# Long convolution of a mixer block by odd frequencies, with time split by four

## The chip, the core and the metric

The kernel runs on one core of one Trainium2 chip. The metric is the device time of one execution in microseconds; the median of three runs before the change is 1589.33 us (1589.04 to 1589.37). Engines: TensorE (PE: matmul; PEld: its weight loads), VectorE (DVE), ScalarE (ACT), GpSimd (POOL) and SyncE (SP, which issues nearly all DMAs). They run side by side and order themselves by semaphores.

## The reference

Two blocks in a row on 512 tokens of width 1024, all in float32. The first has two layers (gated attention, then retention, each with a memory cross-attention). The second mixes the tokens by a gated long convolution (half of its width) and by gated linear attention (the other half), and then runs an MLP. What the change touches is the long convolution, its filter spectrum, and the two norms in a row between the blocks:

```python
def _long_conv(u, spec, bias):
    length = u.shape[1]                      # 512
    uf = u.astype(jnp.float32)
    y = jnp.fft.irfft(jnp.fft.rfft(uf, n=2 * length, axis=1) * spec, n=2 * length, axis=1)[:, :length]
    return (y + uf * bias.astype(jnp.float32)).astype(u.dtype)

def _hyena_gate_conv(u, spec, bias):
    x0, x1, v = jnp.split(u, 3, axis=-1)
    return x0 * _long_conv(x1 * v, spec, bias)

# in _hyena_spectrum: h is the learned filter, 512 taps forward (h[:, 0]) and 512 backward (h[:, 1])
    kern = jnp.concatenate([h[:, 0], jnp.zeros((1, D_HYENA), f32), h[:0:-1, 1]], axis=0)
    kern = kern * lax.rsqrt(jnp.sum(kern * kern, axis=0, keepdims=True) + EPS)
    return jnp.fft.rfft(kern, axis=0)

# first_block ends with rmsnorm(x, final_norm_g); second_block begins with _rms_norm of that
```

## The kernel before, in words

Activations lie transposed: features on the 128 partitions, 512 tokens along the free axis. Every projection walks through the weight matrices in tiles of 128 x 1024 that SP loads into `raw`, three tiles deep behind the split. A float32 product is made of three fp32r products: ACT rounds a weight tile to its high half `wh`, and POOL (or, for the tiles listed in `DVE_LOW`, DVE) makes the low half `wl = raw - wh`; activations are split in the same way (`HH`, `HL`). `features` (L492) then runs per 128 output columns eight matmuls with `wh`, waits for `wl` ("low"), and runs four with it. `unit_f` is two such tiles, 48 matmuls of 512 columns. `feed.take()` and `feed.split_next()` fix, on every engine alike, at which place in its own instruction stream a tile is split: the order on each engine is written out by hand, and each engine works strictly in that order.

Around the change the order on PE is: the last projection of the first block; the transform of the filter (`phases("filter", ...)`, L902 to L919) with the two sums of squares for the norms between them; the units `hx1 0`, `hv 0`, `hx1 1`, `hv 1`, `hx0 0` (projections of the convolution's three inputs, with the turning of u = x1 * v in between); the transform of u for frequencies 0 to 127 (`phases("u", ..., 0, ...)`); the context's sum of squares; unit `hx0 1`; the transform of u for frequencies 128 to 255; the units `og 0` and `gq 0`; the inverse transform (L956 to L966); the gate columns (`slot_gates`, L969, which write banks 4 and 5); and `both_k`, which runs 24 matmuls on the latent tokens and then 24 on the context into bank 4. The latter wait until ACT has copied the gate columns out of bank 4 (`GR`, L2665).

The transform treats even and odd tokens apart (two phases, cosine and sine each), so the filter's and u's transforms are 48 matmuls each, plus four one-row matmuls for the highest frequency. ACT and DVE copy the filter's spectrum to `KS`. DVE then multiplies u's spectrum, which it reads straight from PSUM (`banks`), with `KS` (L1874), adds parts, and POOL adds the rest (L2986, L2988) into `Y`, from which PE takes the inverse: 32 plain float32 matmuls of 256 columns, which the trace shows as 64 records. Behind the products DVE's stream goes on with the context's second norm (`normed("ctx", ...)`: `T<-CX,gxc,R`, then `CL`), ACT's with its high half `CH`, then the splits of the next weight tiles, then `hyena_out(0..3)` (which frees the banks 4 to 7 of the inverse), then `GR`.

The norm between the blocks: ACT makes 1/sqrt of the first sum (`R`), DVE squares it and multiplies the second sum, ACT takes the second 1/sqrt, DVE multiplies the two to `R2`.

Of the kernel before, what the change touches and what calls it, by code (L numbers as in the profile page):

```python
# [8 lines left out]
ALU = mybir.AluOpType  # L9
# [15 lines left out]
QSCALE = 1.0 / math.sqrt(128.0)  # L25
LOGS, TANHS = "natural_log_exp_and_others", "exp_and_others"
# [238 lines left out]
def build(nc, a, out, stack):  # L265
# [49 lines left out]
    one = eps[:, 1:2]  # L315
# [52 lines left out]
    FTH, FTL = at("FTH", [128, 4, 2, 256], 124, F32R), at("FTL", [128, 4, 2, 256], 132, F32R)  # L368
    FTR, IT = at("FTR", [128, 4, 2, 256], 60), at("IT", [128, 2, 2, T], 132)
# [3 lines left out]
    KS = at("KS", [128, 8, T], 140)  # L373
# [7 lines left out]
    TM = [at("TM%d" % n, [128, T], 116 + 2 * n) for n in range(4)]  # L381
# [86 lines left out]
    def tensor(pe):  # L468
# [418 lines left out]
        def phases(tag, x_cos, x_sin, ft, banks, which=range(4)):  # L887

            for n in which:
                (xh, xl), cs, k0 = ((x_cos, 0, 0), (x_cos, 0, 2), (x_sin, 1, 0), (x_sin, 1, 2))[n]  # L890
                b, c = banks[n], slice(128 * ft, 128 * ft + 128)
                pe.wait_ge(done("dft high", 1), *free[b])
                for k in (k0, k0 + 1):
                    mm(bank[b], FTH[:, k, cs, c], xh[:, k, :], k == k0, False)
                    mm(bank[b], FTH[:, k, cs, c], xl[:, k, :], False, False)
                pe.wait_ge(done("dft low"))
                for k in (k0, k0 + 1):
                    i = mm(bank[b], FTL[:, k, cs, c], xh[:, k, :], False, k == k0 + 1)
                i.then_inc(*by_pe("spectrum", tag, ft, n))

        pe.wait_ge(done("energy", 3), done("taps low", 3))
        phases("filter", (URH, URL), (USH, USL), 0, SP_BANKS[0], (0, 1))  # L902
        feed.split_next()
        pe.wait_ge(done("squared", "x2"), *free[6])
        mm(bank[6], ones[:, :], ACC[:, :], True, True).then_inc(*by_pe("sum", "x2"))
        free[6] = (done("sum kept", "x2"),)
        pe.wait_ge(done("squared", "x2 gf"), *free[7])
        mm(bank[7], ones[:, :], ACC2[:, :], True, True).then_inc(*by_pe("sum", "x2 gf"))
        free[7] = (done("sum kept", "x2 gf"),)
        phases("filter", (URH, URL), (USH, USL), 0, SP_BANKS[0], (2, 3))  # L910
        phases("filter", (URH, URL), (USH, USL), 1, SP_BANKS[1])
        for ft in range(2):
            for n in range(4):
                free[SP_BANKS[ft][n]] = (done("spectrum kept", ft, n),)
        pe.wait_ge(*free[4])
        for k in range(2):
            mm(bank[4][0:1, :], FTH[:, k, 1, 0:1], URH[:, k, :], k == 0, False)
            i = mm(bank[4][0:1, :], FTH[:, k, 1, 0:1], URL[:, k, :], False, k == 1)
        i.then_inc(*by_pe("even sum"))  # L919
        free[4] = (done("even sum kept"),)  # L920

        def turn_u(c):
            b = 2 + c
            pe.wait_ge(done("u", c), *free[b])
            for k in range(4):
                ut = UT[:, c, :].rearrange("p (n two) -> p two n", two=2)[:, k // 2, 128 * (k % 2):128 * (k % 2) + 128]
                i = turn(bank[b][:, 128 * k:128 * k + 128], ut)
            i.then_inc(*by_pe("u turned", c))
            free[b] = (done("uk", c),)
# [13 lines left out]
        phases("u", (UKH, UKL), (UKH, UKL), 0, HY_BANKS[0])  # L943
        pe.wait_ge(done("squared", "ctx"), *free[4])
        mm(bank[4][:, 0:256], ones[:, :], ACC[:, 0:256], True, True).then_inc(*by_pe("sum", "ctx"))
        free[4] = (done("sum kept", "ctx"),)
        for b in HY_BANKS[0]:
            free[b] = (done("product", 0),)
        unit_f(("hx0", 1))
        phases("u", (UKH, UKL), (UKH, UKL), 1, HY_BANKS[1])  # L950
        for b in HY_BANKS[1]:
            free[b] = (done("product", 1),)
        feed.split_next()
        unit_f(("og", 0), (2, 3))
# [280 lines left out]
    def vector(dve):  # L1235
# [152 lines left out]
        eng.memset(eps[:, 0:1], 1e-6).then_inc(*by_dve())  # L1388
# [341 lines left out]
        def dft_low():  # L1730
            dve.wait_ge(done("dft"), done("half", ("out", 1, 3), 1, 1))
            for i in range(2):
                dve.wait_ge(done("dft high", i))
                tt(FTL[:, 2 * i:2 * i + 2, :, :], FTR[:, 2 * i:2 * i + 2, :, :], FTH[:, 2 * i:2 * i + 2, :, :].bitcast(F32),
                   ALU.subtract).then_inc(*by_dve("dft low"))

        def filter_norm():
            dve.wait_ge(done("energy scale"))
            ts(chs, chs, 4.0 / 1024.0, None, ALU.mult).then_inc(*by_dve("filter scale"))
# [11 lines left out]
        project_out(1, steps)  # L1751
        x2_done = by_dve.last()
# [9 lines left out]
        def keep_spectrum(ft):  # L1762
            for n in (1, 3):
                dve.wait_ge(done("spectrum", "filter", ft, n))
                eng.tensor_copy(KS[:, 4 * ft + n, :], bank[SP_BANKS[ft][n]]).then_inc(*by_dve("spectrum kept", ft, n))

        def normed(tag, src, gain, scale, n, bias, xh, xl):


            def low(k):  # L1770
                t = temp("normed", tag, k)
                dve.wait_ge(done("h", tag, k), done("even sum") if tag == "x2" and k > 3 else None)
# [14 lines left out]
        t = turn("second scale")  # L1787
        dve.wait_ge(done("scale", "x2"), temp_free("second scale"))
        tt(t[:, :], R[:, :], R[:, :], ALU.mult).then_inc(*by_dve())
        dve.wait_ge(by_dve.last(), done("sum", "x2 gf"))  # L1790
        tt(t[:, :], bank[7], t[:, :], ALU.mult).then_inc(*by_dve("sum kept", "x2 gf"))
        keep_spectrum(0)
        dve.wait_ge(done("second scale"))
        tt(R2[:, :], R2[:, :], R[:, :], ALU.mult).then_inc(*by_dve())
        dve.wait_ge(by_dve.last(), x2_done)
        normed("x2", X, gfx, R2, T, mod, HH, HL)
        keep_spectrum(1)
        dve.wait_ge(done("even sum"), done("spectrum kept", 0, 2))
        eng.tensor_copy(KS[0:1, 2, :], bank[4][0:1, :]).then_inc(*by_dve("even sum kept"))
        def scale_x(ks):  # L1800
            for k in ks:
                stt(X[:, k, :], X[:, k, :], P("gf", k), R[:, :], ALU.mult, ALU.mult).then_inc(*by_dve())
# [45 lines left out]
        tm = [0]  # L1848

        def product(ft, banks):  # L1850

            even_c, odd_c, even_s, odd_s = (bank[b] for b in banks)
            kec, koc, kes, kos = (KS[:, 4 * ft + n, :] for n in range(4))
            dve.wait_ge(*(done("spectrum kept", ft, n) for n in range(4)), done("even sum kept"), done("even sum"))
            for n, parts in ((2, ((even_c, kes, 0), (even_s, kec, 2), (odd_c, kos, 1), (odd_s, koc, 3))),
                             (3, ((even_c, kos, 0), (even_s, koc, 2), (odd_c, kes, 1), (odd_s, kec, 3))),
                             (0, ((even_c, kec, 0), (odd_c, koc, 1), (even_s, kes, 2), (odd_s, kos, 3))),
                             (1, ((even_c, koc, 0), (odd_c, kec, 1), (even_s, kos, 2), (odd_s, kes, 3)))):
                y, made, t = Y[:, 4 * ft + n, :], [], []
                for i, (b, k, from_phase) in enumerate(parts):  # L1860
                    if i == 2 and n % 2 == 0:
                        dve.wait_ge(*made)
                        tt(y, y, t[0], ALU.add).then_inc(*by_dve("y half", ft, n))
                    dve.wait_ge(done("spectrum", "u", ft, from_phase))
                    if i == 0:
                        x = y
                    else:
# [1473 lines left out]
```

## Time and profile before

| | us |
|---|---|
| median of the runs (3) | 1589.33 |
| the profiled execution, own time | 1589.16 |
| its span (first to last instruction) | 1587.4 |
| PE busy | 1578.8 (99%) |
| DVE busy | 995.3 (63%) |
| ACT busy | 725.2 (46%) |
| POOL busy | 602.6 (38%) |

Busy times are sums over the instructions of one engine, with overlaps taken once. Matmuls are pipelined: a record of 0.39 us starts 0.23 us after the one before it, so PE's pace is read from the starts. The result of a matmul reaches the other engines at the end of its record.

### The profile page before, as it was taken

How to read it: one execution, taken by the hardware profiler on the slowest of the kernel's cores; microseconds unless marked ns; L12 is line 12 of the kernel's file. 1: busy time of each engine (PE TensorE's matmuls, PEld its weight loads, DVE VectorE, ACT ScalarE, POOL GpSimd, SP SyncE). 2: the span in 40 equal slices, each digit the busy share in tenths (PEclk: the TensorE clock that was granted, in tenths of full speed). 3: DMA queues.
4: the chain of work that ended last, by engine and by line, in shares of the span. 5: the costliest groups of instructions: out<-in, count | busy, mean ns of one | idle time of the engine just before them, and what ended most of it. 6: DMA issues, size and time to landing. Idle time of an engine off the chain costs nothing.

```text
span 1587.4 us, 21833 instructions
## 1 busy us (share of the span) xinstructions
PE 1578.8 (99%) x8864; PEld 1360.0 (86%) x8864; DVE 995.3 (63%) x1479; ACT 725.2 (46%) x1116; POOL 602.6 (38%) x301
## 2 busy tenths in 40 slices
PE   9999999999999999999999999999999999999998
PEld 7888898889888888888888778889888889999997
DVE  7888867676766365554554676782356885555554
ACT  6533443343433344455555554324434555545454
POOL 1002113221244434455555443353223335555552
PEclk9999999999999999999999999999999999999999
DMA  6554434343466423333333432132111233233321
GB/s 246 171 174 147 141 119 136 117 132 127 121 221 201 164 69 106 102 100 106 107 107 104 148 124 66 54 107 83 41 54 67 80 106 107 94 106 95 105 93 54
DMA packets 54413, 182.69 MB, mean 115 GB/s; under 512 B 6556, under 2 KB 7196, under 8 KB 53928
## 3 DMA queue, kind: packets, MB, share of 16 engines
q1 hardware_dynamic: 54024, 180.76, 34.6%
q8 instruction: 70, 1.15, 0.3%
q10 hardware_dynamic: 288, 0.52, 0.1%
q14 instruction: 31, 0.25, 0.1%
HBM read 174.16 MB, written 3.96 MB: 112 GB/s over the span
## 4 chain that ended last, share of the span: by engine, by line
PE 94%; DVE 4%; DMA 0%; ACT 0%; issue 0%; SPq 0%; POOL 0%; DVEq 0%; ACTq 0%
PE banks L472 92%; PE banks L475 2%; DVE ada L1242 1%; DVE wl L1273 1%; DMA maskf<-cst_dram 0%; DVE WA L1242 0%; DVE TM L1874 0%; ACT Sc L2221 0%; DVE ACC L1309 0%; DVE TM L1884 0%; DVE nmx L1345 0%; POOL wl L2896 0%; DVE Sc L1355 0%; DVE ML L1242 0%; SPq L3072 0%
## 5 line engine op out<-in xcount | busy, mean ns | idle before, releaser
L2896 POOL TENSOR_TENSOR wl<-raw,wh 128x1024 fp32r<-128x1024 f32 x139 | 346.0, 2492 | 383.3 <-ACT wh L2224 383.3
L472 PE MATMUL banks<-HH,wh 128*128 128x512 f32 (+2 forms) x944 | 362.1, 386 | 0.3 <-DVE X L1550 0.3
L472 PE MATMUL banks<-HL,wh 128*128 128x512 f32 (+2 forms) x944 | 352.6, 379 | 0.0
L2224 ACT ACTIVATE wh<-raw 128x1024 fp32r<-128x1024 f32 x246 | 257.2, 1051 | 190.6 <-PE banks L472 182.7
L472 PE MATMUL banks<-HH,wl 128*128 128x512 f32 (+1 forms) x936 | 251.2, 380 | 0.1
L472 PEld LDWEIGHTS banks<-HH,wh 128*128 128x128 f32 (+1 forms) x944 | 177.2, 188 | 37.0 <-issue 2.6
L472 PEld LDWEIGHTS banks<-HL,wh 128*128 128x128 f32 (+1 forms) x944 | 177.0, 188 | 34.5 <-issue 1.2
L472 PEld LDWEIGHTS banks<-HH,wl 128*128 128x128 f32 x936 | 172.1, 188 | 35.0 <-issue 1.5
L472 PE MATMUL banks<-wh,HH 128*128 128x256 f32 x448 | 127.8, 285 | 0.0
L472 PE MATMUL banks<-wl,HH 128*128 128x256 f32 x448 | 126.7, 283 | 0.0
L472 PE MATMUL banks<-wh,HL 128*128 128x256 f32 x448 | 126.7, 283 | 0.0
L1273 DVE TENSOR_TENSOR wl<-raw,wh 128x1024 fp32r<-128x1024 f32 x82 | 100.4, 1237 | 23.5 <-ACT wh L2224 23.5
L472 PE MATMUL banks<-OH,wh 128*128 128x512 f32 x256 | 101.6, 397 | 0.0
L472 PE MATMUL banks<-FLO,wh 128*128 128x512 f32 x256 | 99.8, 390 | 0.0
L472 PE MATMUL banks<-OL,wh 128*128 128x512 f32 x256 | 99.8, 390 | 0.0
L472 PE MATMUL banks<-FHI,wh 128*128 128x512 f32 x256 | 99.7, 390 | 0.0
L2909 POOL TENSOR_TENSOR OL<-T,OH 128x512 fp32r<-128x512 f32 x21 | 28.0, 1335 | 178.4 <-ACT OH L2224 178.4
L472 PEld LDWEIGHTS banks<-wh,HL 128*128 128x128 f32 x448 | 85.7, 191 | 0.5 <-issue 0.2
L472 PEld LDWEIGHTS banks<-wh,HH 128*128 128x128 f32 x448 | 85.7, 191 | 0.5 <-issue 0.2
L472 PEld LDWEIGHTS banks<-wl,HH 128*128 128x128 f32 x448 | 85.7, 191 | 0.0
L2901 POOL TENSOR_TENSOR SL<-WS,SH 128x1024 fp32r<-128x1024 f32 x24 | 57.9, 2412 | 46.1 <-ACT SH L2224 46.1
L2934 POOL TENSOR_TENSOR CM<-CB,mask 128x512 f32<-128x512 f32 x12 | 27.6, 2297 | 124.0 <-DMA CB<-sums_dram 115.8
(441 smaller groups left out, 3262.0 us busy)
## 6 DMA issues: line engine op xcount, KB each, us to landing
raw<-wst_dram SPq DMA_DIRECT2D x294, 512.0 KB, 3.5
X<-xT_dram SPq DMA_DIRECT2D x8, 512.0 KB, 6.0
CB<-sums_dram SPq DMA_DIRECT2D x12, 256.0 KB, 3.1
D<-dec_dram SPq DMA_DIRECT2D x12, 256.0 KB, 2.8
x_dram<-X SPq DMA_DIRECT2D x3, 512.0 KB, 6.7
QS<-QX SPq DMA_DIRECT2D x24, 64.0 KB, 2.8
KSw<-KX SPq DMA_DIRECT2D x24, 64.0 KB, 2.0
X<-x_dram SPq DMA_DIRECT2D x3, 512.0 KB, 4.5
```

The source lines that it names most:

```text
L472: return pe.eng.matmul(dst, w, x, start=start, stop=stop, skip_group_check=True)
L475: return pe.eng.transpose(dst, x, ident[:, :])
L1242: return eng.scalar_tensor_tensor(out=dst, in0=x, scalar=s, in1=y, op0=op0, op1=op1)
L1273: tt(wl[:, q, :], raw[:, i % NRAW, :], wh[:, q, :].bitcast(F32), ALU.subtract).then_inc(*by_dve("low", u))
L2224: return eng.activation(dst, src, ACT.Copy)
L2896: tt(wl[:, q, :], raw[:, i % NRAW, :], wh[:, q, :].bitcast(F32), ALU.subtract).then_inc(*by_pool("low", u))
L2901: tt(SL_[:, v % NS, :], WS[:, v % 2, :], SH_[:, v % NS, :].bitcast(F32), ALU.subtract).then_inc(*by_pool("sums low", u))
L2909: tt(OL[:, tile, :], t[:, :], OH[:, tile, :].bitcast(F32), ALU.subtract).then_inc(*by_pool("l", "o", l, tile))
L2934: tt(CM[:, :].rearrange("p (i m) -> p i m", i=4), CB[:, :].rearrange("p (i m) -> p i m", i=4), mask[:, :].rearrange("p (i m) -> p i m", i= ...
```

## The change

The transform now takes 256 odd frequencies of a length of 2048 half steps, f = 2k + 1, and the tokens in four groups by their number modulo 4. A matmul of one group gives 128 frequencies, and the other 128 follow from sums and differences of the groups. So the filter's transform is 36 matmuls (`spectrum(...)`, one or two groups each) and that of u 24, both before unit `hx0 1`; u's second transform behind `hx0 1` is gone. The inverse is 32 float32 matmuls of 128 columns. In return there are sums and differences ahead of the product and behind it. ACT copies one of two bank pairs to `TM` or `HO`, DVE adds and subtracts (`XP`, `Y`), POOL makes the filter's sums in `KS` (`filter_pair`), the differences `XM` (in `Y`), a part of the last product and the odd parts. The products are made of tiles 1024 long whose two inputs both lie in SBUF (`XP` or `XM`, and `KS`). For the inverse, the groups 0 and 2 of all four channel tiles come first, then 1 and 3.

Unit `hx0 1` writes banks 6 and 7 in place of 0 and 1; the context's sum of squares goes to bank 2, between the halves of `hx0 1`, and is taken out by ACT behind that unit's `conv`. Unit `og 0`, which is next, writes banks 2 and 3.

For the two norms, DVE forms the weighted sum ACC2 + 1e-6 ACC before the sum over partitions, and ACT takes R2 from that one sum (bias 1e-12).

```diff
+        def spectrum(b, *terms):
+            pe.wait_ge(done("dft high"), *free[b])
+            for n, (m, (xh, xl), p) in enumerate(terms):
+                mm(bank[b], FTH[:, m, :], xh[:, p, :], n == 0, False)
+                mm(bank[b], FTH[:, m, :], xl[:, p, :], False, False)
+            pe.wait_ge(done("dft low"))
+            for n, (m, (xh, xl), p) in enumerate(terms):
+                i = mm(bank[b], FTL[:, m, :], xh[:, p, :], False, n == len(terms) - 1)
...
+        pe.wait_ge(done("both squared", "x2"), *free[7])
+        mm(bank[7], ones[:, :], ACC2[:, :], True, True).then_inc(*by_pe("sum", "x2 gf"))
...
+        def context_sum():
+            pe.wait_ge(done("squared", "ctx"), *free[2])
+            mm(bank[2][:, 0:256], ones[:, :], ACC[:, 0:256], True, True).then_inc(*by_pe("sum", "ctx"))
+            free[2] = (done("sum kept", "ctx"),)
+
+        unit_f(("hx0", 1), (6, 7), beside=context_sum)
         feed.split_next()
         unit_f(("og", 0), (2, 3))
         unit_f(("gq", 0))
+        for group in ((0, 2), (1, 3)):
+            for c in range(4):
...
+                for p in group:
+                    pe.wait_ge(done("y", p))
+                    for cs in range(2):
+                        i = mm(bank[b][:, 128 * p:128 * p + 128], Z[p][:, cs, 128 * c:128 * c + 128], IT[:, p, cs, :],
+                               p + cs == 0, p == 3 and cs == 1)
...
+        dve.wait_ge(done("squared", "x2"), done("squared", "x2 gf"))
+        stt(ACC2[:, :], ACC[:, :], EPS, ACC2[:, :], ALU.mult, ALU.add).then_inc(*by_dve("both squared", "x2"))
...
+        def times(sign, b):
+            x, p, q = (XP, XM)[sign], (PP, PM)[sign][:, 2 * b:2 * b + 2, :], TM[:, 2 * b:2 * b + 2, :]
+            h = KS[:, 4 * sign + 2 * b:4 * sign + 2 * b + 2, :]
+            dve.wait_ge(done("h", b), done(("x plus", "x minus")[sign], b))
+            for n, dst in enumerate((p, q)):
                 dve.wait_ge(by_dve.last())
+                tt(dst, x[:, 2 * b + n:2 * b + n + 1, :].to_broadcast([128, 2, T]), h, ALU.mult).then_inc(*by_dve("times", sign, b))
...
         for j in range(2):
-            conv(("hx0", 1), j, j, 2 + j, X0[:, 2 + j, :])
+            conv(("hx0", 1), j, 6 + j, 2 + j, X0[:, 2 + j, :])
+        rstd(done("sum", "ctx"), ("sum kept", "ctx"), ("scale", "ctx"), 2, 256, R[:, 0:256], 1024, done("x2 scaled"))
```

POOL's stream from the filter's transform to the inverse, before. `wl` is the low half of a weight tile, `Y` the product, `TM` a part of it:

```order
L2896 TENSOR_TENSOR wl<-raw,wh 128x1024 x25
L2988 TENSOR_TENSOR Y<-Y,TM_168 128x512
L2986 TENSOR_TENSOR Y<-Y,TM_166 128x512
L2988 TENSOR_TENSOR Y<-Y,TM_167 128x512
L2988 TENSOR_TENSOR Y<-Y,TM_166 128x512
L2986 TENSOR_TENSOR Y<-Y,TM_168 128x512
L2988 TENSOR_TENSOR Y<-Y,TM_169 128x512
L2896 TENSOR_TENSOR wl<-raw,wh 128x1024 x3
```

Six more such additions and the gate columns' tile follow. The same stretch after the change, where `KS` is the filter's spectrum, `Y<-Y` makes the differences of u's parts, and `PP` is the product of the sums:

```order
L2894 TENSOR_TENSOR wl<-raw,wh 128x1024 x17
L2976 TENSOR_TENSOR KS<-KS,TM 128x1024
L2977 TENSOR_TENSOR KS<-KS,TM 128x1024
L2894 TENSOR_TENSOR wl<-raw,wh 128x1024 x2
L2976 TENSOR_TENSOR KS<-KS,HO 128x1024
L2977 TENSOR_TENSOR KS<-KS,HO 128x1024
L2894 TENSOR_TENSOR wl<-raw,wh 128x1024 x7
L2988 TENSOR_TENSOR Y<-Y 128x1024 x2
L2894 TENSOR_TENSOR wl<-raw,wh 128x1024 x2
L2993 TENSOR_TENSOR Y<-Y,TM 128x512
L2994 TENSOR_TENSOR Y<-Y,TM 128x512
L2997 TENSOR_TENSOR Y<-PP,Y 128x512
```

The 28 low halves are all still there; four instructions for the filter came in ahead, and of the product's part two long ones stand before the low halves of `og 0`'s second and `gq 0`'s first tile, five instructions (the last one 1024 long) behind them.

DVE's stream before, from the middle of the first product (its inputs are `banks`, in PSUM, and `KS`):

```order
L1874 TENSOR_TENSOR Y<-banks,KS 128x512
L1874 TENSOR_TENSOR TM_166<-banks,KS 128x512
L1874 TENSOR_TENSOR TM_167<-banks,KS 128x512
L1874 TENSOR_TENSOR TM_168<-banks,KS 128x512
L1884 TENSOR_TENSOR TM_167<-TM_167,TM_168 128x512
```

After the change, the stretch from the conv of `hx0 1` to the context's norm:

```order
L1253 SCALAR_TENSOR_TENSOR X_165<-banks,par,X_165 128x8x63 x4
L1865 TENSOR_TENSOR Y<-Y,KS 128x1024
L1865 TENSOR_TENSOR TM<-Y,KS 128x1024
L1865 TENSOR_TENSOR Y<-Y,KS 128x1024
L1865 TENSOR_TENSOR TM<-Y,KS 128x1024
L1870 TENSOR_TENSOR Y<-Y,TM 128x512
L1871 TENSOR_TENSOR Y<-Y,TM 128x512
L1284 TENSOR_TENSOR wl<-raw,wh 128x1024
L1888 TENSOR_TENSOR XP<-PP,Y 128x1024 x2
L1890 TENSOR_TENSOR TM<-XP 128x1024
L1891 TENSOR_TENSOR TM<-XP 128x1024
L1893 TENSOR_TENSOR Y<-Y 128x1024
```

The products no longer read PSUM, and the low half that DVE makes for the second tile of `gq 0` (`wl`, L1284) stands behind all of them; before, it stood among the last products.

## Rows read from the trace of the kernel before

**Rows 1.** The page: busy times, the clock granted to PE, the chain that ended last

```profile
PE 1578.8 (99%) x8864; PEld 1360.0 (86%) x8864; DVE 995.3 (63%) x1479; ACT 725.2 (46%) x1116; POOL 602.6 (38%) x301
PEclk9999999999999999999999999999999999999999
PE 94%; DVE 4%; DMA 0%; ACT 0%; issue 0%; SPq 0%; POOL 0%; DVEq 0%; ACTq 0%
```

**Rows 2.** Windows: start:end, length, busy time of each engine (instructions), PEclk, DMA, GB/s

```profile
942.35:955.92 13.57, 13.57 (x57) 10.10 (x56) 10.45 (x20) 7.96 (x12) 2.38 (x1) 1.00 0.43 150
955.92:966.80 10.88, 10.88 (x49) 9.01 (x48) 8.85 (x13) 5.55 (x9) 2.33 (x1) 1.00 0.00 0
```

**Rows 3.** Timeline of PE (start, length, instructions): inverse, narrow float32 matmuls, norm sums

```profile
1056.92 13.97 PE L472 MATMUL banks<-IT,Y 128*128 128x256 f32 x64
1070.55 0.58 PE L472 MATMUL banks<-HH,wh 128*64 128x512 f32 x1
...
1124.92 1.95 PE L472 MATMUL banks<-LG,MS 128*128 128x128 f32 x16
1126.70 0.39 PE L472 MATMUL banks<-LC,MS 128*128 128x128 f32 x2
...
945.07 1.88 PE L472 MATMUL banks<-ACC,ones 128*128 128x512 f32 x4
```

**Rows 4.** Timeline of DVE around the norm sums: squares, then the second norm

```profile
943.94 1.30 DVE L1309 TENSOR_TENSOR ACC<-ACC,T 128x512 f32<-128x512 f32 x2 [0.70 <-ACT T L2221]
951.38 1.42 DVE L1242 SCALAR_TENSOR_TENSOR T<-X,gfx,R 128x512 f32<-128x512 f32 x2
```

**Rows 5.** Timeline of ACT: conv of a unit, root of the context's sum

```profile
1012.76 0.78 ACT L2221 ACTIVATE X<-banks,par 128x512 f32<-128x512 f32 x1 [1.92 <-PE banks L472]
1018.63 0.47 ACT L2221 ACTIVATE R<-banks,eps 128x256 f32<-128x256 f32 x1 [5.09 <-PE banks L472]
```

**Rows 6.** Timelines of DVE and POOL where both read from SBUF

```profile
922.55 0.69 DVE L1728 TENSOR_TENSOR URL<-UR,URH 128x512 fp32r<-128x512 f32 x1
923.15 2.88 DVE L1728 TENSOR_TENSOR USL<-US,USH 128x512 fp32r<-128x512 f32 x1
...
922.94 2.54 POOL L2896 TENSOR_TENSOR wl<-raw,wh 128x1024 fp32r<-128x1024 f32 x1 [2.94 <-ACT wh L2224]
...
1037.09 2.58 DVE L1863 TENSOR_TENSOR Y<-Y,TM 128x512 f32<-128x512 f32 x1
1039.60 1.27 DVE L1874 TENSOR_TENSOR TM<-banks,KS 128x512 f32<-128x512 f32 x2
1040.91 1.58 DVE L1884 TENSOR_TENSOR TM<-TM,TM 128x512 f32<-128x512 f32 x1
...
1036.73 5.21 POOL L2896 TENSOR_TENSOR wl<-raw,wh 128x1024 fp32r<-128x1024 f32 x2
1042.57 1.30 POOL L2988 TENSOR_TENSOR Y<-Y,TM 128x512 f32<-128x512 f32 x1 [0.63 <-DVE TM L1884]
```

**Rows 7.** Instructions by tile, durations in ns min/median/max: a DVE pass 1024 long

```profile
L1734 DVE TENSOR_TENSOR FTL<-FTR,FTH x2: 1217/1218/1218, 931.3 to 932.4; 128x1024 fp32r<-128x1024 f32 x2
```

**Rows 8.** Timelines of DVE, ACT and PE from the end of the products to `both_k`

```profile
1053.83 1.91 DVE L1242 SCALAR_TENSOR_TENSOR T<-CX,gxc,R 128x256 f32<-128x256 f32 x2
...
1063.89 0.73 ACT L2221 ACTIVATE T<-banks,tq 128x512 f32<-128x512 f32 x1
1077.66 0.57 ACT L2224 ACTIVATE GR<-banks 64x512 f32<-64x512 f32 x1
...
1081.73 0.28 PE L472 MATMUL banks<-wh,CH 128*128 128x256 f32 x1
```

**Rows 9.** PE's last work (timeline), then windows behind it (columns as in rows 2)

```profile
1579.04 2.82 PE L475 MATMUL banks<-ident,XG 128*128 128x128 f32 x24
...
1585.00:1586.00 1.00, 0.00 (x0) 0.00 (x0) 0.00 (x0) 0.00 (x0) 0.00 (x0) 1.00 1.06 406
1586.00:1587.00 1.00, 0.00 (x0) 0.00 (x0) 0.00 (x0) 0.00 (x0) 0.00 (x0) 0.82 0.49 186
```

More of the change, by code:

```diff
@@ L906, in tensor @@
         free[6] = (done("sum kept", "x2"),)
[L907 to L920, printed above, removed]
+        spectrum(0, (COS_OF[1], ur, 1), (COS_OF[3], ur, 3))
+        spectrum(1, (SIN_OF[1], us, 1), (SIN_OF[3], us, 3)).then_inc(*by_pe("filter odd", 0))
+        spectrum(6, (SIN_OF[1], ur, 1), (LESS_SIN_3, ur, 3))
+        spectrum(7, (COS_OF[3], us, 3), (LESS_COS_1, us, 1)).then_inc(*by_pe("filter odd", 1))
+        free[2] = free[3] = (done("even copied"),)
+        free[4] = free[5] = (done("even made"),)
+        free[0] = free[1] = (done("odd kept", 0),)
+        free[6] = free[7] = (done("odd kept", 1),)
         def turn_u(c):
@@ L1786, in vector @@
         feed.split_next()
[L1787 to L1795, printed above, removed]
+        dve.wait_ge(done("even copied"), done("filter even", 1))
+        tt(KS[:, 4:6, :], TM[:, 0:2, :], psum[:, 4:6, :], ALU.add).then_inc(*by_dve())
+        tt(KS[:, 6:8, :], TM[:, 0:2, :], psum[:, 4:6, :], ALU.subtract).then_inc(*by_dve("even made"))
+        dve.wait_ge(done("second scale"), x2_done, done("gains"))
         normed("x2", X, gfx, R2, T, mod, HH, HL)
-        keep_spectrum(1)
-        dve.wait_ge(done("even sum"), done("spectrum kept", 0, 2))
-        eng.tensor_copy(KS[0:1, 2, :], bank[4][0:1, :]).then_inc(*by_dve("even sum kept"))
         def scale_x(ks):
+            dve.wait_ge(done("scale", "x2"))
             for k in ks:
@@ L1898, in vector @@
         feed.split_next()
-        product(1, HY_BANKS[1])
+        for b in (1, 0):
+            times(1, b)
+        times_summed(1, 0)
+        feed.split_next()
         feed.unit()
+        dve.wait_ge(done("product", 1, 0), done("product", 1, 1))
+        for b in (0, 2):
+            tt(XP[:, b:b + 2, :], PP[:, b:b + 2, :], PM[:, b:b + 2, :], ALU.add).then_inc(*by_dve("even parts"))
+        dve.wait_ge(by_dve.last())
+        tt(Z[0], XP[:, 0:2, :], XP[:, 2:4, :], ALU.add).then_inc(*by_dve("y", 0))
@@ L2555, in dft_high @@
         def dft_high():
[L2556 to L2558 removed]
+            act.wait_ge(done("dft"), done("half", ("out", 1, 3), 1, 1))
+            copy(FTH[:, :, :], FTR[:, :, :]).then_inc(*by_act("dft high"))
         def filter_norm():
@@ L2622, in scalar @@
                 conv(("hx1", half), j, o + j, 4 + 2 * half + j, X1[:, j, :], done("sum", "x2"), done("energy", 3),
-                     done("even sum"), done("sum", "x2 gf"), done("u", 1) if half else None)
+                     done("filter odd", 1), done("sum", "x2 gf"), done("u", 1) if half else None)
             if half:
```

259 lines of the change are left out of this document (115 added, 144 removed).

## The prediction

> **What bounds the kernel now.** I read the page first: PE is busy 99% of the span, nearly all of the chain that ended last is PE, and its clock is full in all slices [rows 1]. Then the timelines of every engine from 940 to 1085 us, where the changed work lies: PE has no hole there, so a matmul taken out is time gained as long as the other engines deliver. 48 matmuls take 10.88 us in one unit [rows 2], 0.227 us each. Last I looked at what DVE, ACT and POOL do between u's transform and the gate columns, since the change gives them work and takes from PE the time in which they did it. Below, all times are on the scale of the old trace, and "ready" is the end of a record plus what the next engine takes to start (0.05 to 0.1 us).
>
> **What PE saves.** The filter: 52 matmuls become 36; u: 48 become 24. 40 x 0.227 = 9.1 us. The inverse: 64 records from 1056.92 to 1070.55, 13.6 us; the new ones are 128 columns wide, and 16 such records of other tiles take 1.78 us (1124.92 to 1126.70), 0.111 each [rows 3], so 7.1 us: 6.5 saved. Together 15.6 us.
>
> **The two norms.** The filter's stage and its two sums last 13.57 us [rows 2]. PE now does 12 matmuls (until 945.07, where the sums began before [rows 3]) and then waits for the weighted sum. DVE ends the two sums of squares at 945.24 [rows 4]; the new instruction behind them needs 0.75 (a T<-X,gfx,R of rows 4 takes that): 946.1. PE idles 1.0 us. Then the sums (1.7) and 24 matmuls (5.4): the stage ends at 953.3, 2.65 earlier. In return ACT has the second root at 948.5 and DVE, behind its two new sums of the even parts, starts the norm at 948.9 rather than 951.38 [rows 4], 2.45 earlier; PE needed HL about 3 us after it was made, so nothing waits. POOL's four new filter sums of 2.4 us fall between low halves that are made 7 to 8 us before PE wants them: no cost. If that cover were gone they would cost up to 9.6.
>
> So u's transform starts at 1009.9 and ends at 1015.35 (24 matmuls).
>
> **The context's sum.** Bank 2 is released by ACT's logarithm, which now stands behind the two convs of `hx0 1`. That unit ends at 1026.7 (two halves and the sum of 0.43 between them). The conv starts 0.16 later and lasts 0.68 until the next instruction, the logarithm 0.47 [rows 5]: bank 2 is free at 1028.05, and `og 0`, whose first matmul writes it, waits 1.35 us. I take this as certain.
>
> **DVE and POOL.** The trace shows that a DVE instruction with two inputs in SBUF and a POOL instruction do not run together. The DVE instruction of 1037.09 takes 2.58 us for 0.69: it ends 0.55 after the end of POOL's first (2.4 of the 5.21 us); POOL's next then ends late by 0.45, and DVE's of 1040.91 takes 1.58 [rows 6]. They take turns, one instruction each. Where DVE's next stands ready at once (923.15), POOL, waiting since 922.94, still gets the turn first, and DVE takes 2.88. The products before read one input from PSUM, and two of them run in 1.27 us beside POOL (1039.60) [rows 6]. After the change all products and nearly all sums have both inputs in SBUF. A turn given to a POOL instruction of 2.4 us costs DVE 2.1 (0.14 overlap at either end), one of 1.3 us costs 1.0.
>
> The Trainium skill, "SBUF — State Buffer", section Who interferes with whom, speaks against this change: a DVE instruction with two SBUF inputs blocks against a POOL instruction that reads SBUF, one with a single SBUF input does not. The trace agrees (1.27 against 2.58 us). The page counts inputs and makes no exception for one that is repeated, as in `times`; by it the sum is the one below, and were repeated inputs exempt, the turns taken between the eight products (about half of them) would go, which is the time of the second rival.
>
> DVE's stream: the first two sums of u run from 1012.85 to 1015.2, the next three wait for ACT's second copy (1015.5 to 1016.6) and end at 1019.1. Then come 17 passes of 1024 (1.21 each [rows 7]: two XP, eight products, the low half for `gq 0`, two XP, four Z make 17), six of 512 (0.69) and the four convs (2.75 in all): 26.9 us with their small overlaps. POOL's turns among them: at the start 0.8 (rest of a low half); the two differences XM and the low halves of `og 0` and `gq 0`, 4 x 2.1; then 4 short ones x 1.0 and the long odd part, 2.1. That is 14.5. In order: first product 1022.3; the four products of the sums end at 1033.5; the convs at 1040.8; the eighth product at 1046.8; **the low half for `gq 0` at 1050.2; first Z at 1058.0; context's norm begins at 1061.3**, against 1053.83 before [rows 8].
>
> **What PE makes of it.** `og 0` 1028.05 to 1038.95; `gq 0`'s second tile starts at 1044.4 and wants its low half 1.8 later, at 1046.2: 4.0 us of waiting. The remaining 16 matmuls end at 1053.9. The inverse waits for Z until 1058.05, 4.1 us, and some 0.7 for the second Z; it ends at 1065.9. The gate columns need their weight tile and bank 4, which both stand behind the context's norm on ACT. ACT's copy out of bank 4 came at 1063.89, 10.06 after the norm's start, of which 1.04 was a turn of POOL (two instructions of 256 in 1.91 us, 0.87 alone) that falls away [rows 8]. So it starts at 1061.3 + 9.0 = 1070.3 and the bank is free at 1071.1: 5.2 us. PE then does gates and the latent half of `both_k` (11.2 us) until 1082.4. The context half wants `GR`'s copy, which ended at 1078.23 [rows 8] and now ends 7.5 - 1.0 later, 1084.7. It started at 1081.73 [rows 8]: **PE is 3.0 us later than before**. What follows had ACT and DVE ahead of PE by more than the 3.5 us by which they have fallen back against it (the next low half is used 3 us after it is ready), so nothing is added or returned.
>
> Check from the other side: saved 15.6, waits 1.0 + 1.35 + 4.0 + 4.8 + 5.2 + 2.3 = 18.65, net +3.05. The profiled execution's own 1589.16 + 3.0 = 1592.2; the median lies 0.17 above it: 1592.3. This chain has some forty links, each known to a few hundredths; I allow 2 us either way.
>
> **Bounds of what the trace does not show.** A product 1024 long with a repeated input: 1.21 [rows 7] to 2 x 0.69 [rows 6]; I take 1.21, the other adds 0.17 x 8 = 1.4. ACT's copy of two banks: 1.07 (two single ones) to 1.2. The write in steps of four: nothing to 0.1 each, 0.4. POOL's turns: from none to all.
>
> **Rivals.**
> 1. DVE and POOL do not disturb each other here. For: the old products ran beside POOL. Against: rows 6. DVE would be done at 1046; waits left are 1.0, 1.35 and about 0.2 at `GR`. 1589.3 - 15.6 + 2.6 = 1576.3. Chance 0.07.
> 2. POOL gets only part of the turns (DVE keeps going where its next instruction is ready). For: in rows 6 only one place shows who wins then. Against: each product waits for the one before it, so POOL is asked first anyway. With half of the 14.5 us the norm starts at 1054 and `GR` is copied at 1077.5; PE's context half then starts near 1077.7: 1585.3. Chance 0.17.
> 3. Slower still: PE's clock falls in the third wait. PE is idle 5.2 us there. At the end of the span the last matmul ends at 1581.9; the clock is full from 1585 to 1586, and the mean of the next microsecond is 0.82 [rows 9], so it fell at about 1586.6, 4.8 us after work ended. At 1.2 GHz the 11.2 us before the context half take up to 22.4, end at 1093.5 instead of 1084.7, and give 1601. It decides only if more than 2.3 us are lost, since the wait for `GR` hides so much; a fall in the first two waits is hidden by the waits behind them. The Trainium skill, "TensorE: Matmul & The Clock Gate", section Why this matters for your kernels, warns of gaps between bursts of matmuls as a cause of the lower clock; by that rule the waits here are a risk, and the sum would be up to 1601. Chance 0.08, most of it between 1593 and 1597.
>
> **How the numbers follow.** The forecast has 0.64, rival 2 0.17, rival 3 0.08, rival 1 0.07; 0.04 is for something unseen. A measurement here can tell 0.2%, 3.2 us, so "within" is 1586.15 to 1592.5, and the forecast lies at its upper edge: of its 0.64 I give 0.34 to slower, 0.30 to within. Slower: 0.34 + 0.08 + 0.02 = 0.44; faster: 0.07 + 0.10 of rival 2 + 0.02 = 0.19; within 0.37. The range leaves out rival 1 and the far end of rival 3: 1583.5 to 1597. The forecast alone has 1590.3 to 1594.5.
>
> **What would show it.** PE waits behind DVE's or ACT's instructions at five places: before the norm sums (1.0), at the first matmul of `og 0` (1.35), for a DVE-made `wl` in `gq 0` (4), before the inverse (4), before the gate columns (5). Products of 1.21 us that show as 3.3 where POOL works beside them. From `hx1 0` to `hx0 0` PE runs 2.65 us early without a hole. I am wrong if the products beside POOL keep 1.2 us, or if `GR`'s copy does not set the start of the context half.

## The result, and the profile after

The changed kernel takes 1595.69 us (median of five runs, 1595.6 to 1595.87), the kernel before in the same comparison 1589.23 (1589.04 to 1589.37). The ratio is 1.0041, with a 95% interval of 1.0029 to 1.0052: it is slower, by 6.5 us. The profiled execution took 1595.6 with a span of 1593.7. The forecast was 1592.3 (1583.5 to 1597), most likely slower: the direction is right, the loss is 6.5 in place of 3.1. The wide range holds the result; the range given for the forecast alone, 1590.3 to 1594.5, is missed by 1.2 us.

The page of the changed kernel, to be read beside [rows 1]: PE is busy 9.6 us less, its share falls, DVE's part in the chain that ended last grows from 4% to 7%, and the row of the clock has one slice below full.

```profile
PE 1569.2 (98%) x8824; PEld 1350.6 (85%) x8824; DVE 1005.6 (63%) x1453; ACT 728.6 (46%) x1116; POOL 617.6 (39%) x300
PEclk9999999999999999999999999989999999999999
PE 90%; DVE 7%; ACT 1%; issue 1%; DMA 0%; SPq 0%; DVEq 0%; ACTq 0%
```

The waits of PE in the changed kernel: engine, line and tile waited for, us in total, how often, the longest. `Z`, 0.6 of `T` and 0.6 of `wl` lie in other stretches and stand in the kernel before as well; the rest is new, as the same view of that kernel lists no wait of PE between 900 and 1100 us.

```profile
PE banks L474 <- ACT T L2215: 5.8, 1, 5.8
PE banks L474 <- DVE wl L1284: 4.8, 2, 4.2
PE banks L474 <- DVE T L1253: 1.6, 2, 1.0
PE banks L474 <- DVE TM L1890: 1.5, 1, 1.5
PE banks L474 <- ACT R L2215: 1.3, 1, 1.3
PE banks L474 <- DVE Z L1402: 1.3, 1, 1.3
PE banks L474 <- DVE ACC L1253: 0.9, 1, 0.9
PE banks L474 <- ACT GR L2218: 0.6, 1, 0.6
PE banks L474 <- ACT UKH L2218: 0.4, 1, 0.4
PE banks L474 <- DVE TM L1891: 0.4, 1, 0.4
```

Windows of the changed kernel (columns as in [rows 2]): the two stretches around the changed work in which PE's granted clock was at 1.2 GHz, half of full.

```profile
1050.97:1057.79 6.82, 5.11 (x12) 4.06 (x13) 6.79 (x5) 0.00 (x0) 6.22 (x3) 0.50 0.23 77
1071.45:1078.27 6.82, 3.96 (x10) 1.89 (x11) 2.94 (x4) 4.44 (x6) 2.89 (x2) 0.50 0.59 196
```

DVE and POOL of the changed kernel beside each other, where the products are (timelines; columns start, length, instruction, idle time before). A product between POOL's instructions takes 3.3 to 3.4 us, one beside an idle POOL 1.23. This answers [rows 6].

```profile
1024.24 3.42 DVE L1865 TENSOR_TENSOR PP<-XP,KS 128x1024 f32<-128x1024 f32 x1
1027.69 3.28 DVE L1865 TENSOR_TENSOR TM<-XP,KS 128x1024 f32<-128x1024 f32 x1
...
1043.02 1.23 DVE L1865 TENSOR_TENSOR Y<-Y,KS 128x1024 f32<-128x1024 f32 x1
1047.98 2.18 DVE L1865 TENSOR_TENSOR TM<-Y,KS 128x1024 f32<-128x1024 f32 x1
...
1024.19 5.70 POOL L2988 TENSOR_TENSOR Y<-Y 128x1024 f32<-128x1024 f32 x2 [2.30 <-DVE XP L1856]
1029.85 3.38 POOL L2894 TENSOR_TENSOR wl<-raw,wh 128x1024 fp32r<-128x1024 f32 x1
```

The places that answer to [rows 3, 8] in the changed kernel (timelines of PE, DVE and ACT): the norm sums, the start of the next unit, the hole at 979, the late low half, first `Z`, gate columns, the context's norm, the copy out of bank 4, and `GR`.

```profile
945.99 1.98 PE L474 MATMUL banks<-ACC,ones 128*128 128x512 f32 x4 [0.86 <-DVE ACC L1253]
953.30 0.39 PE L474 MATMUL banks<-HH,wh 128*128 128x512 f32 x1
979.00 0.50 PE L474 MATMUL banks<-HH,wh 128*128 128x512 f32 x1 [1.01 <-DVE T L1253]
1052.68 2.08 PE L474 MATMUL banks<-HH,wl 128*128 128x512 f32 x4 [4.20 <-DVE wl L1284]
1060.51 0.68 PE L474 MATMUL banks<-IT,TM 128*128 128x128 f32 x4 [1.54 <-DVE TM L1890]
1074.31 0.66 PE L474 MATMUL banks<-HH,wh 128*64 128x512 f32 x1 [5.79 <-ACT T L2215]
...
1063.69 0.87 DVE L1253 SCALAR_TENSOR_TENSOR T<-CX,gxc,R 128x256 f32<-128x256 f32 x2
...
1072.99 1.18 ACT L2215 ACTIVATE T<-banks,tq 128x512 f32<-128x512 f32 x1
1087.26 0.57 ACT L2218 ACTIVATE GR<-banks 64x512 f32<-64x512 f32 x1
```

PE begins the context half of `both_k` at 1087.88, 6.15 us later than before (1081.73, [rows 8]); its last matmul ends 6.33 later. So nearly all of the loss is made by then.

A new sum over PE's path, from the starts of matmuls (each hole is the distance between two starts less 0.23). Saved 15.6 by the forecast's count. Lost: norm sums 1.0; holes at 979.0 and 988.8, 1.2 + 0.4; `og 0` 1.5; late low half 4.4; `Z` 1.7 + 0.4; gate columns 5.8; `GR` 0.7; and the clock: in the two stretches at 1.2 GHz matmuls start 0.43 us apart in place of 0.23, which costs 2.5 + 1.9. That is 21.5, net +5.9 where 6.15 is measured. What is left, 0.25, is of the size of what the sum leaves out: the matmul after the first one behind a wait starts 0.31 to 0.34 us after it and not 0.23 (979.00 to 979.34, 1030.08 to 1030.39).

### The profile page after: what moved, and what is told of

The parts are those of the page before. It is cut to its first block, busy times and chain, and to the rows that moved or that the text cites. A ratio compares the mean times of both kernels' runs of the same rounds, so it can differ in the third digit from the quotient of the medians.

```text
span 1593.7 us, 21727 instructions
## 1 busy us (share of the span) xinstructions
PE 1569.2 (98%) x8824; PEld 1350.6 (85%) x8824; DVE 1005.6 (63%) x1453; ACT 728.6 (46%) x1116; POOL 617.6 (39%) x300
## 4 chain that ended last, share of the span: by engine, by line
PE 90%; DVE 7%; ACT 1%; issue 1%; DMA 0%; SPq 0%; DVEq 0%; ACTq 0%
PE banks L474 88%; PE banks L477 2%; DVE wl L1284 1%; DVE ada L1253 1%; DVE T L1253 1%; DVE TM L1865 1%; DVE WA L1253 0%; DMA maskf<-cst_dram 0%; ACT T L2215 0%; DVE PP L1865 0%; DVE XP L1888 0%; DVE ACC L1320 0%; ACT Sc L2215 0%; DVE Y L1865 0%; ACT wh L2218 0%
## 5 line engine op out<-in xcount | busy, mean ns | idle before, releaser
L1284 DVE TENSOR_TENSOR wl<-raw,wh 128x1024 fp32r<-128x1024 f32 x82 | 101.0, 1245 | 24.0 <-ACT wh L2218 24.0
```

The source lines that it names most:

```text
L1284: tt(wl[:, q, :], raw[:, i % NRAW, :], wh[:, q, :].bitcast(F32), ALU.subtract).then_inc(*by_dve("low", u))
```

## Theories

Mine after the traces: from u's transform on, PE's path is slack. What decides is one chain: PE's end of u's transform, then DVE's products with POOL's turns between them, the context's norm, ACT's four copies, `GR`. Every wait of PE inside that stretch, and the falls of the clock, only fill slack; what makes the chain longer counts in full. Then most of the 3.4 us that the forecast lacks are two holes of PE ahead of u's transform (1.6), 0.5 more in DVE's chain and 0.7 on ACT. The chain that ended last in the changed kernel (start, length, what; the pieces left out are DVE's and ACT's and the short gaps between them) has no piece of PE from the end of u's transform to the start of the context half:

```profile
1006.47 10.95 PE banks L474 x48
1017.44 1.04 ACT TM L2218
...
1087.35 0.49 ACT GR L2218
...
1087.88 22.24 PE banks L474 x152
```

The rival is the bookkeeping of the sum above: each wait is a cost of its own, and the one removed is gained. A second rival concerns the turns: the products are slow by their repeated input or by traffic to SBUF in general, and not by the number of inputs there. Each experiment was timed beside the kernel before. Where an experiment is compared with the changed kernel or with another experiment, it is by medians, each over runs that spread by 0.5 to 0.8 us where no range is given.

## Experiments

**Norm change alone (norm_only).** The kernel before, with:

```diff
+        stt(ACC2[:, :], ACC[:, :], 1e-6, ACC2[:, :], ALU.mult, ALU.add).then_inc(*by_dve("both squared", "x2"))
-        tt(t[:, :], R[:, :], R[:, :], ALU.mult).then_inc(*by_dve())
-        tt(t[:, :], bank[7], t[:, :], ALU.mult).then_inc(*by_dve("sum kept", "x2 gf"))
-        tt(R2[:, :], R2[:, :], R[:, :], ALU.mult).then_inc(*by_dve())
```

> The kernel before, with the change of the two norms alone (weighted sum ACC2 + 1e-6 ACC ahead of the sum over partitions, the second root straight from it). My theory: PE waits about 1.0 us for the weighted sum ahead of the norm sums, where it waited for nothing, and the norm that starts earlier on DVE gives nothing back, because PE wants HL about 3 us after it is made. So the time rises by 1.0 us, to 1590.2 us. Rival: the earlier norm lets PE run on somewhere later, or the wait is absorbed by one behind it: 1589.2 us or less.

Measured 1590.54 against 1589.33, ratio 1.0007 (0.9999 to 1.0016): +1.2 us, with an interval that just holds no change. The trace has the wait of 0.86 ahead of the norm sums and none that went in return. A simplification that replaces three DVE instructions by one costs about 1 us by the medians, because it puts that one in front of PE and shortens a way that nobody waited for.

**POOL's filter sums later (late_pair).**

```diff
         filter_pair(0)
-        units(1)
+        units(3)
         filter_pair(1)
-        units(3)
+        units(1)
```

> The changed kernel, with POOL's second pair of filter sums (KS<-KS,HO, two instructions of 2.4 us) two units later in POOL's stream. My theory: those two and the low halves that they push back make DVE's UT<-T,X take 2.61 us at 974.9 and the scalings X<-X,par,R 2.9 us each at 980 and 984, and so keep banks from PE twice (holes of 1.2 us at 979.0 and 0.4 us at 988.8); the whole chain from u's transform to the context half of both_k hangs on the time at which PE ends u's transform, so both holes count in full: 1595.7 - 1.6 = 1594.1 us. Rival: PE waits for other engines five times further on, and one of these waits swallows the 1.6 us: 1595.7 us.

Measured 1593.95, ratio 1.0029 (1.0018 to 1.0040): 1.7 below the changed kernel; both holes are gone. DVE in the changed kernel, then in this one (timelines):

```profile
974.91 2.61 DVE L1832 TENSOR_TENSOR UT<-T,X 128x512 f32<-128x512 f32 x1
980.21 7.02 DVE L1253 SCALAR_TENSOR_TENSOR X<-X,par,R 128x512 f32<-128x512 f32 x4
```

```profile
975.01 0.69 DVE L1832 TENSOR_TENSOR UT<-T,X 128x512 f32<-128x512 f32 x1
980.03 2.73 DVE L1253 SCALAR_TENSOR_TENSOR X<-X,par,R 128x512 f32<-128x512 f32 x4
```

POOL's low halves were ahead of PE by enough to bear the four filter sums; DVE's instructions beside them were not. These came late, and with them the banks that PE wanted.

**The wait ahead of `og 0` (root_first).** `rstd(...)` for the context stands ahead of the two `conv` of `hx0 1` on ACT.

> The changed kernel, with ACT's root of the context's sum ahead of the two convs of hx0 1 in place of behind them. PE's wait of 1.5 us ahead of og 0 (1028.6 to 1030.1) goes. My theory: that wait is not on the path that sets the end; DVE's chain of products decides from u's transform on until the context half of both_k, and PE will wait 1.5 us longer for the low half in gq 0 (4.4 + 1.5): no change, 1595.7 us. Rival (the sum of PE's waits, as the prediction's sum was written): every wait counts, 1594.2 us.

Measured 1595.78, ratio 1.0040 (1.0028 to 1.0053): no change. The 1.5 us reappear in the wait for DVE's low half (5.8 for 4.2), and `both_k`'s context half starts at 1087.75 (1087.88 in the changed kernel). PE's longest waits in this kernel:

```profile
PE banks L474 <- DVE wl L1284: 6.4, 2, 5.8
PE banks L474 <- ACT T L2215: 4.2, 1, 4.2
```

The bookkeeping rival, which forecast 1594.2, falls.

**Contiguous writes (read_steps).**

```diff
-fn(t.rearrange("p (n four) -> p four n", four=4), bank[4 + c].rearrange("p (four n) -> p four n", four=4), ...
+fn(t.rearrange("p (n four) -> p n four", four=4), bank[4 + c].rearrange("p (four n) -> p n four", four=4), ...
```

> The changed kernel, where ACT's four copies out of the inverse's banks write one token after the other and read the bank in steps of 128 columns, in place of writing in steps of four tokens and reading in a row. My theory: the write in steps is what makes a copy take 1.15 to 1.19 us where it took 0.78 before; then the copies take 0.78, GR's copy comes 4 x 0.4 = 1.6 us earlier and bank 4 is free 0.4 us earlier; PE's path through the gate columns (0.4 earlier, 0.7 of waiting for GR gone) allows 1.1 us: 1594.6 us. Rival: a step on the reading side costs the same, or the copies are not on the path: 1595.7 us.

Measured 1595.45, ratio 1.0040 (1.0027 to 1.0052): 0.24 below, where 1.1 was expected. This kernel's runs (1595.35 to 1596.14) enclose those of the changed kernel, so the times alone show no gain; in the trace the context half starts 0.43 us earlier (1087.45 for 1087.88). The size of the write in steps was right, as the instructions of tile `T` show (durations in ns, min/median/max): before, changed, this one.

```profile
L2221 ACT ACTIVATE T<-banks,tq x4: 707/712/732, 1063.9 to 1073.4; 128x512 f32<-128x512 f32 x4
```

```profile
L2215 ACT ACTIVATE T<-banks,tq x4: 1153/1167/1187, 1073.0 to 1083.0; 128x512 f32<-128x512 f32 x4
```

```profile
L2215 ACT ACTIVATE T<-banks,tq x4: 669/670/683, 1073.1 to 1082.6; 128x512 f32<-128x512 f32 x4
```

The copies do lie on the chain, but that their saving goes through in full was wrong. In this kernel (timelines), DVE's instruction behind the third copy starts while POOL works, and then takes 1.30, where the same behind the second copy takes 0.74:

```profile
1077.22 0.74 DVE L1253 SCALAR_TENSOR_TENSOR T<-UT,par,T 128x512 f32<-128x512 f32 x1
1079.97 1.30 DVE L1253 SCALAR_TENSOR_TENSOR T<-UT,par,T 128x512 f32<-128x512 f32 x1 [1.27 <-ACT T L2215]
...
1079.43 1.29 POOL L3004 TENSOR_TENSOR YL<-T,YH 128x512 fp32r<-128x512 f32 x1 [4.79 <-ACT YH L2218]
```

The instructions behind the first and the fourth copy also meet POOL (1.40 and 1.30); in the changed kernel the four take 0.91, 0.75, 0.82 and 0.83. That takes back 1.4 of the 2.0 us that the faster copies save, and `GR` comes only 0.44 earlier, 1086.82 for 1087.26.

**One input of the products in PSUM (sums_in_banks).**

```diff
+        xs = (psum[:, 4:6, :], psum[:, 0:2, :])
-            tt(XP[:, b:b + 2, :], Y[:, b:b + 2, :], Y[:, 4 + b:6 + b, :], ALU.add)
+            tt(xs[b // 2], Y[:, b:b + 2, :], Y[:, 4 + b:6 + b, :], ALU.add)
```

> The changed kernel, where DVE writes the sums XP of u's parts to PSUM (banks 4, 5 and 0, 1, which are free then) in place of SBUF, so that its first four products read one input from PSUM and one from SBUF; all else is as it was. My theory (a DVE instruction with both inputs in SBUF and a POOL instruction take turns; one with an input in PSUM runs beside POOL): the four products take 1.2 us each in place of 3.3, 8.4 us less; POOL then makes its two differences at its own pace, but its two low halves fall beside DVE's four sums of the products, which still read SBUF twice, and cost two turns of 2.1 there. Left are 4.2 us: 1595.7 - 4.2 = 1591.5 us. Rival 1: the turns come from traffic to SBUF in general, whatever the number of inputs; the products stay at 3.3 us and the time at 1595.7. Rival 2: the products are slow by their repeated input and not by POOL; they stay at 3.3 us as well, also where POOL is idle.

Measured 1591.73, ratio 1.0015 (1.0006 to 1.0024): 4.0 below the changed kernel. The trace has four products of 1.23 beside POOL, and the turns where they were expected, in two of the sums whose inputs are both in SBUF:

```profile
1024.29 1.23 DVE L1867 TENSOR_TENSOR PP<-banks,KS 128x1024 f32<-128x1024 f32 x1
1028.14 1.22 DVE L1867 TENSOR_TENSOR TM<-banks,KS 128x1024 f32<-128x1024 f32 x1
1029.28 2.61 DVE L1872 TENSOR_TENSOR PP<-PP,TM 128x512 f32<-128x512 f32 x1
1031.82 2.88 DVE L1873 TENSOR_TENSOR PP<-PP,TM 128x512 f32<-128x512 f32 x1
```

The repeated input is still there, so it is not what made the products slow; nor is SBUF traffic in general, since the same results are written and `KS` is still read there. Both second rivals fall. The rule of the Trainium skill that the prediction weighed ("SBUF — State Buffer", section Who interferes with whom: two SBUF inputs block, one does not) holds here, the repeated input counted as an input.

**The second products and their sums too (products_in_banks).** The second product of each pair goes to `xs[b]` in place of `TM`, and the sums read it there.

> As sums_in_banks, and the second product of each pair (TM before) goes to the same PSUM banks in place, so that the four sums behind the products have one input in PSUM too. My theory: neither the four products nor their sums wait for POOL; the eighth product ends some 8.4 us earlier (1041.7 for 1050.2), the norm of the context starts that much earlier (1055.3), and GR is copied at 1079.4 in place of 1087.8. PE no longer waits for the low half in gq 0, and still 6 us for the gate columns: 1595.7 - 8.4 = 1587.3 us, below the kernel before. Rival: what is saved is taken back by the waits that stay (PE itself needs its 11.2 us behind the gate columns' bank, and the clock falls in the one long wait): 1590 to 1592 us.

Measured 1587.56, ratio 0.9989 (0.9980 to 0.9998), 8.1 below the changed kernel. DVE's sums run in 0.68 beside POOL's low halves:

```profile
1029.42 0.68 DVE L1872 TENSOR_TENSOR PP<-PP,banks 128x512 f32<-128x512 f32 x1
1031.21 0.68 DVE L1873 TENSOR_TENSOR PP<-PP,banks 128x512 f32<-128x512 f32 x1
...
1029.09 4.91 POOL L2896 TENSOR_TENSOR wl<-raw,wh 128x1024 fp32r<-128x1024 f32 x2
```

**POOL's differences on DVE (differences_dve).** The two `XM` of POOL are made by DVE, behind the two `XP`.

> The changed kernel, with the two differences XM made by DVE (two more instructions 1024 long) in place of POOL. My theory: a turn of POOL's 2.4-us instruction costs DVE 2.1, its own instruction for the same costs 1.2, so DVE's chain gets 2 x 0.9 = 1.8 us shorter although it has more to do: 1593.9 us. Rival (no turns are taken, DVE's chain is as long as what DVE has to do): 2 x 1.2 longer: 1598.1 us.

Measured 1593.89, ratio 1.0028 (1.0017 to 1.0039), 1.8 below: DVE has 2.4 us more to do and its chain is shorter, so what counts is the turns and not the sum of DVE's work.

**Three places mended (three_mended).** `products_in_banks`, `late_pair`, and `spectrum(0, ...)` ahead of the two norm sums.

> products_in_banks with two more edits: POOL's second pair of filter sums two units later (as in late_pair), and 6 matmuls of the filter's transform (bank 0) put ahead of the two norm sums, so that the weighted sum is ready when PE comes to it (banks 7 and 6 then written in this order). My theory: all three mended places lie on the path of their own, so the savings add: 1587.6 - 1.7 (late_pair's) - 1.0 (PE's wait ahead of the norm sums) = 1584.9 us. Rival: the roots now come 0.4 us later than PE can hide, or one of the places was only on the path because of another: 1585.9 or more.

Measured 1585.19, ratio 0.9973 (0.9963 to 0.9984), 2.4 below products_in_banks. The savings add, to within 0.3 us.

**ACT's stream reordered (act_moved).**

```diff
-        normed_high("ctx", 256, modc, CH)
-        feed.unit()
         for j in range(2):
             act.wait_ge(done("unit", ("gq", 0), j))
             fn(qT[:, j, :], bank[j], ACT.Copy, scale=0.125).then_inc(*by_act("kept", ("gq", 0), j))
+
+        normed_high("ctx", 256, modc, CH)
+        feed.take()
...
+            if c == 0:
+                feed.take()
...
-        for c in range(4):
+        for c in range(3):
             hyena_out(c)
...
-        feed.take()
...
+        hyena_out(3)
+        feed.take()
```

`feed.take()` is the split of a weight tile; the copies of `GR` and `GC` stand between the loop and `hyena_out(3)`.

> three_mended with ACT's stream reordered: the two copies qT out of banks 0 and 1 ahead of the context's norm (1.2 us), the second weight split behind the first copy out of the inverse (1.0 us), GR's and GC's copies ahead of the last hyena_out. My theory: PE's wait for bank 4 ahead of the gate columns (5.8 us in products_in_banks) is all that stands on the path behind the inverse, and PE is bound from there: 2.2 us less, 1582.7 us; if the granted clock no longer falls in the shorter wait (it was at 1.2 GHz from 1065.0 to 1071.7 in products_in_banks, which cost 2.75 us of PE), 2.75 less still: 1579.9 us. Rival: ACT's idle time ahead of the norm is not there, or the earlier gate columns only wait for the context's norm (CH) instead: 1584.9 us.

Measured 1582.56 (1581.84 to 1583.8), ratio 0.9958 (0.9945 to 0.9970), 2.6 below three_mended. PE's wait for bank 4 fell from 5.8 to 3.9, and its clock still fell. What each of the three moves gives by itself was not tried.

**The clock by itself (filled, split_first, filled_split_first).** In `filled`, 12 matmuls whose result is overwritten unused fill the wait of `act_moved`. The split ahead of the last `hyena_out` is the one difference of the other two from `act_moved` and `filled`.

> act_moved with 12 matmuls of 512 columns between the inverse and the gate columns, whose result in bank 0 is overwritten unused: 2.7 us of work in a wait of some 3.6 us. It separates the wait from the clock. If the clock still falls in act_moved, this one keeps it at 2.4 GHz and is 2.7 us faster than it: 1579.9 us. If it doesn't fall there, or what is lost by it is hidden by a later wait, both are equal. If the fillers end behind the time at which bank 4 is free, this one is slower by the difference, at most 2.7 us.

> act_moved with the split of the weight tile for both_k's second half ahead of the last hyena_out on ACT. PE waited for no such tile in act_moved, so my theory says no change: 1582.5 us. Rival: the reordering itself moves the time (the last hyena_out is now later and POOL's low half meets other DVE instructions): 1581.5 or 1583.5 us.

> split_first with the 12 filling matmuls of filled. In filled the clock stayed at 2.4 GHz, but PE then waited twice for the weight tile whose split stood behind the last hyena_out (0.53 us for ACT's high half, 0.53 for POOL's low half), which took the gain away: 1582.1 against 1582.5. With these waits gone the gain of the clock must show: my theory 1582.5 - 1.3 = 1581.1 us, 1.0 to 1.5 below split_first. Rival (the clock does not matter, or a further wait swallows it): equal to split_first.

`filled` 1582.08 (1581.94 to 1582.84; ratio 0.9955, 0.9942 to 0.9967): the clock stayed full, and most of the gain went into two new waits of 0.53; the 0.5 us to `act_moved` lie within the spread of both. `split_first` 1582.21 (1580.9 to 1583.2; ratio 0.9955, 0.9942 to 0.9969): no change. `filled_split_first` 1580.67 (1580.52 to 1581.66; ratio 0.9947, 0.9934 to 0.9959): 1.5 below split_first. The runs of the two overlap (1580.9 to 1583.2 against 1580.52 to 1581.66), so I go by the traces, one of each: windows of split_first, then of filled_split_first.

```profile
1059.00:1061.00 2.00, 0.00 (x0) 0.00 (x0) 1.47 (x4) 1.59 (x4) 0.45 (x1) 1.00 0.00 0
1061.00:1063.00 2.00, 1.33 (x5) 0.76 (x6) 1.41 (x2) 1.38 (x2) 0.82 (x2) 0.86 0.36 92
1063.00:1065.00 2.00, 2.00 (x6) 0.87 (x5) 1.30 (x2) 1.73 (x2) 2.00 (x1) 0.50 0.42 170
```

```profile
1059.00:1061.00 2.00, 1.99 (x9) 1.31 (x7) 1.78 (x5) 1.42 (x4) 0.01 (x1) 1.00 0.00 0
1063.00:1065.00 2.00, 2.00 (x10) 1.07 (x9) 1.30 (x2) 1.49 (x2) 2.00 (x1) 1.00 0.60 240
```

From the first matmul of the gate columns to the last of the kernel it is 512.8 us in split_first (1061.67 to 1574.50) and 511.2 in filled_split_first (1062.11 to 1573.35): 1.6 us for the clock, which in split_first was at 1.2 GHz from 1062.4 to 1065.8. The fillers let the gate columns start 0.44 us later, so 1.1 of the 1.6 us is left in these two executions. This version is 8.6 us faster than the kernel before and 15.0 faster than the changed one, and still uses the transform with odd frequencies. That is not what the transform is worth: the new order of ACT's stream and the other mended places were not tried in the kernel before.

## Why the prediction was right in its direction and short in its size

- **Which path gave the result.** The measured 1595.7 lies between 1593 and 1597, where rival 3 had most of its chance, but not by its mechanism: the clock fell in the third wait and cost PE 1.9 us, less than the 2.3 that rival 3 needed, and PE still waited 0.7 for `GR`. The loss that the forecast lacks came from elsewhere, as below; that the wide range holds it is in part luck.
- **What PE saves: right.** The stage of the filter ends at 953.30, predicted 953.3, and PE idles the predicted 1.0 us in it.
- **"From hx1 0 to hx0 0 PE runs 2.65 us early without a hole", "POOL's four new filter sums ... no cost": this step failed.** I asked whether POOL's low halves would be late and not what DVE does while POOL works. Two holes, 1.6 us by the trace; late_pair gives back 1.7. The same happened ahead of the first norm, where it cost nothing: DVE's two small `gx` instructions at 945.86 took 2.40 us beside a low half of POOL, and the norm began at 950.63, not at 948.9.
- **The context's sum: right in size** (1.5 for 1.35), and worth nothing, as root_first shows. The forecast lists it among the costs, but its times already let the wait behind it shrink by as much.
- **DVE and POOL take turns: right.** Shown by sums_in_banks, products_in_banks and differences_dve within 0.3 us each. The times came late: first product 1024.24 (predicted 1022.3), eighth product's end 1050.16 (1046.8), low half's end 1052.6 (1050.2), norm of the context 1063.69 (1061.3). Of the 2.4 us at the norm, 1.9 were there at the first product. The eighth product's end was 3.4 late because two of POOL's short turns fell among the last four products and not one; behind them one fewer came, and the low half was 2.4 late again. The forecast's 14.5 us of turns leave out the 0.8 at the start that stands in its own list; its times contain it.
- **ACT's copies: the term was mis-sized.** I allowed 0.1 us for the write in steps of four; it is 0.46 (1.17 for 0.71). Norm to `GR`'s end took 24.1 us where 23.4 were foreseen. Yet mending it brings `GR` only 0.44 us forward and shows no gain clear of the spread in the time, since POOL's turns come to lie beside it.
- **The clock (rival 3): the estimate of when it falls was wrong, it had no part in the result.** I placed the fall 4.8 us after work ended; it came 2.5 and 2.9 us after the end of PE's last matmul (1048.48 and 1068.52; windows above). It cost PE 4.4 us of pace, and all of it was hidden: PE waits again behind each fall (1.7 for `Z` and 5.8 for bank 4 behind the first, 0.7 for `GR` behind the second). The first fall is also why the wait for `Z` was 1.7 us where 4.1 were forecast. Where the chain had been shortened until PE was the bound, it did count, 1.6 us of one fall. The Trainium skill, "TensorE: Matmul & The Clock Gate", section Why this matters for your kernels, warns of gaps between bursts of matmuls; the traces agree, with falls in the waits of 4.2 and 5.8 us here.
- Together, at the start of the context half: 3.0 as predicted, 1.9 up to the first product (1.6 of it the holes), 0.5 on DVE, 0.7 on ACT: 6.1 for 6.15 measured. Of the 0.3 beside the holes 0.2 are the slower second matmul behind two of the waits (945.99, 979.00); how the rest and the 0.5 on DVE come about stays open.

## What to carry to other kernels

Moving work off the engine that is the bound is worth nothing if it lands on two engines that then exclude each other: count for every instruction of DVE that gets two SBUF inputs the turns of POOL beside it, over the whole stretch and for work that is not part of the change as well. If banks are free, put one of the inputs into PSUM; here that took 8.1 us off with no instruction less. And in a stretch where PE waits several times, look for the one chain that decides: waits ahead of it are exchanged for waits behind it.

## What the hardware showed beyond the forecast

- In-place products in PSUM (`banks<-banks,KS`, 1024 long, one input repeated) take 1.23 us, as those in SBUF beside an idle POOL.
- ACT's copy of 128x512 writing SBUF in steps of four elements takes 1.17 us, in steps of two (the kernel before) 0.71, and 0.67 where it reads PSUM in steps of 128 elements and writes in a row.
- How long PE had been idle when its clock fell differs: 2.5 and 2.9 us in the changed kernel, 4.5 in products_in_banks (the last matmul of the inverse ends at 1060.43; windows below), 4.8 and 2.1 behind the last matmul of the kernel before and of the changed one. In split_first the clock fell at 1062.4, 4.6 us after the last matmul's end and 0.8 after PE had resumed work (window 1061.00:1063.00 above). So the length of the wait alone does not tell whether it falls.

```profile
1064.00:1065.00 1.00, 0.00 (x0) 0.00 (x0) 0.00 (x0) 1.00 (x4) 0.88 (x1) 0.97 0.09 29
1065.00:1066.00 1.00, 0.00 (x0) 0.00 (x0) 0.00 (x0) 1.00 (x2) 1.00 (x1) 0.50 0.94 319
```
